# One decoder trunk step on one core: last up products stored after one tile load, three word gathers per two row gathers, a fourth row buffer, the residual read back in four larger transfers

## The reference

```python
s1, i1 = lax.top_k(s[:, :, 0], 16); s2, i2 = lax.top_k(s[:, :, 1], 16)   # 8 heads, 128 keys a side
...                                                    # the best 16 of the 256 pairs of a head
act = jax.nn.gelu(jnp.einsum('cd,chkd->chk', hc, expert_u[idx]))
return jnp.einsum('chk,chkd->cd', gate * act, expert_v[idx])
```

## Time and profile before

| | us |
|---|---|
| median of 3 runs (lowest, highest) | 2215.64 (2212.16, 2217.15) |
| the profiled execution's own time | 2217.63 |
| its span, first to last instruction | 2215.9 |
| TensorE busy | 2166.3 (98%), x16578 |
| VectorE busy | 1620.5 (73%) |
| ScalarE busy | 1120.8 (51%) |
| GpSimd busy | 785.4 (35%) |
| mean granted TensorE clock | 0.988 of full speed |

### The profile page before, as it was taken

How to read it: one execution, slowest core, us unless ns; L and a number is a source line. 1 busy time by engine, 2 the same in 40 slices (tenths; PEclk the granted TensorE clock), 3 DMA queues, 4 the chain that set the end, 5 groups by cost and what they waited for, 6 DMA issues and landing times.

```text
span 2215.9 us, 53111 instructions
## 1 busy us (share of the span) xinstructions
PE 2166.3 (98%) x16578; PEld 2128.9 (96%) x16578; DVE 1620.5 (73%) x2983; ACT 1120.8 (51%) x2094; POOL 785.4 (35%) x612
## 2 busy tenths in 40 slices
PE   9999999999999999999999999999889999999997
PEld 8999899999999999999999999999789999999997
DVE  8778688886766767888885444466567787788886
ACT  6445366667455445555555444455333444444453
POOL 0321100002011000888888888200577433222231
PEclk9999999999999999999999999999999999999998
DMA  7887656666556556877776878698899999899995
GB/s 245 292 292 248 224 185 199 207 210 209 182 187 204 176 173 182 192 179 190 189 185 179 204 185 188 179 314 260 273 320 307 350 390 379 313 369 371 369 365 191
DMA packets 303834, 546.01 MB, mean 246 GB/s; under 512 B 77072, under 2 KB 116456, under 8 KB 303600
## 3 DMA queue, kind: packets, MB, share of 16 engines
q1 hardware_dynamic: 227024, 427.68, 59.6%
q0 software_dynamic: 60064, 105.07, 16.0%
q10 hardware_dynamic: 16640, 12.06, 1.8%
HBM read 519.39 MB, written 25.28 MB: 246 GB/s over the span
## 4 chain that ended last, share of the span: by engine, by line
PE 65%; POOL 5%; issue 3%; DMA 2%; DVE 2%; ACT 0%; DVEq 0%; SPq 0%; ACTq 0%
PE ps L317 15%; PE ps L320 15%; PE ps L316 15%; PE ps L2207 8%; PE ps L2220 5%; PE ps L2211 5%; POOL gu L1790 3%; DMA gat<-expert_v,gidx 2%; POOL gat L1639 1%; DVE lo L1623 0%; PE ps L2251 0%; DMA raw<-weights 0%; PE ps L1403 0%; DMA gu<-u_spill,gidx 0%; DVE gacc L2085 0%
## 5 line engine op out<-in xcount | busy, mean ns | idle before, releaser
L304 DVE TENSOR_TENSOR lo<-raw,hi 128x512 fp32r<-128x512 f32 x995 | 685.8, 697 | 365.6 <-ACT hi L299 345.0
L299 ACT CAST hi<-raw 128x512 fp32r<-128x512 f32 x995 | 608.1, 620 | 471.9 <-PE ps L320 447.2
L316 PE MATMUL ps<-h_hi,hi 128*128 128x264 f32 (+1 forms) x3200 | 821.8, 286 | 1.0 <-DVE h_lo L957 1.0
L317 PE MATMUL ps<-h_lo,hi 128*128 128x264 f32 (+1 forms) x3200 | 820.1, 286 | 0.0
L316 PEld LDWEIGHTS ps<-h_hi,hi 128*128 128x128 f32 x3200 | 601.8, 188 | 7.9 <-issue 6.3
L317 PEld LDWEIGHTS ps<-h_lo,hi 128*128 128x128 f32 x3200 | 602.0, 188 | 0.3 <-issue 0.2
L1773 POOL DMA_INDIRECT w_spill<-chosen,widx x256 | 432.4, 1689 | 264.5 <-DVE widx L1998 186.8
L320 PE MATMUL ps<-h_hi,lo 128*128 128x264 f32 (+1 forms) x3200 | 523.3, 285 | 2.1 <-DVE lo L304 1.9
L320 PEld LDWEIGHTS ps<-h_hi,lo 128*128 128x128 f32 x3200 | 444.3, 188 | 3.8 <-DVE lo L304 3.6
L2207 PE MATMUL ps<-whl,hi 128*128 128x368 f32 x1544 | 348.7, 348 | 6.4 <-DVE whl L2077 5.2
L1639 POOL DMA_INDIRECT gat<-expert_v,gidx x160 | 178.0, 1112 | 315.4 <-DVE gacc L2085 297.4
(11 more groups left out here) (308 smaller groups left out, 2294.4 us busy)
## 6 DMA issues: line engine op xcount, KB each, us to landing
raw<-u_tiles SPq DMA_DIRECT2D x512, 256.0 KB
raw<-weights SPq DMA_DIRECT2D x480, 256.0 KB
raw_v<-expert_v SPq DMA_DIRECT2D x128, 512.0 KB
raw<-expert_v SPq DMA_DIRECT2D x124, 512.0 KB
w_spill<-zeros ACTq DMA_DIRECT2D x16, 736.0 KB, 5.6
wld<-w_spill SPq DMA_DIRECT2D x32, 368.0 KB, 4.1
u_spill<-ust SPq DMA_DIRECT2D x128, 40.0 KB
qb<-q_spill POOLq DMA_DIRECT2D x8, 512.0 KB, 5.9
```

Source lines behind the costliest of these rows:

```text
L299: nc.scalar.copy(hi[k % SPLIT][:], raw_quarter(k)).then_inc(hi_done, 1)
L304: nc.vector.tensor_tensor(lo[k % SPLIT][:], raw_quarter(k), hi[k % SPLIT][:].bitcast(F32), ALU.subtract).then_inc(lo_done, 1)
L316: pe.matmul(out, a, rhs[0][:, first + j, 0:n], start=start and j == 0, stop=False)
L317: pe.matmul(out, a, rhs[1][:, first + j, 0:n], start=False, stop=False)
```

## The change

- SyncE stores the last up products behind the load of tile 4 of round 0, ahead of those of tiles 5 to 7.
- A fourth row buffer `gat3`, over the third cell buffer of `wld`; row n goes out when add n-4 is done. Before row 3, the first into that buffer, GpSimd waits until VectorE's multiplications of the up pass are done.
- GpSimd's list: five words; then two words behind each of rows 0 to 4; from row 5 one behind an odd row and two behind an even one.
- Five batches of words: up to word 5, 15, 30, 50, 80, weighed ahead of rounds 1, 2, 4, 7, 10.
- Adds of the first pass: round 1 has four (behind k=3, 5, 6, 7), rounds 2 to 7 five, rounds 8 to 13 six, 14 and 15 five.
- The residual comes back in four transfers of 528 KB: one behind the loads of round 1's tiles, one behind round 2's, two behind round 3's.
- Five semaphores that are only counted up become one, `go`.

```diff
+    gat3 = place("gat3", at["raw_v"] + 2 * 4 * 4 * TD, [P, HALF * P])
+    gacc = place("gacc", at["gat3"], [P, len(GROUPS), HALF * P])
...
-    gat.append(gat2)
+    gat += [gat2, gat3]
+    ROWS = len(gat)
...
-    BOUNDS = (1, 3, 6, 9)
+    BOUNDS = (1, 2, 4, 7, 10)
     FIVE, SIX = (1, 2, 3, 5, 6), (1, 2, 3, 5, 6, 7)
-    ADDS = [[()] + 7 * [FIVE] + 4 * [SIX] + [SIX, FIVE, FIVE, (0, 1, 2, 3, 4)], 15 * [FIVE] + [(0, 1, 2, 3, 4)]]
+    ADDS = [[(), (3, 5, 6, 7)] + 6 * [FIVE] + 6 * [SIX] + [FIVE, (0, 1, 2, 3, 4)], 15 * [FIVE] + [(0, 1, 2, 3, 4)]]
+    WORDS_AT = (0, 5, 15, 30, 50, TG)
...
-        for s in range(RAW, SLOTS):
+        def x2_back(q):
+            at_q = slice(4 * q, 4 * q + 4) if isinstance(q, int) else bass.ds(4 * q, 4)
+            sp.dma_start(x2[:, at_q], x2_dram[:, at_q]).then_inc(x2_in, 16)
+        load_expert(0, 0, RAW)
+        spill(PAIR_U - 1, 1)
+        for s in range(RAW + 1, SLOTS):
             load_expert(0, 0, s)
-        spill(PAIR_U - 1, 1)
...
-        sp.dma_start(x2[:, 0], x2_dram[:, 0]).then_inc(x2_in, 16)
-        sp.dma_start(x2[:, KD - 1], x2_dram[:, KD - 1]).then_inc(x2_in, 16)
-        for first, last in ((1, CHUNKS - UP_CHUNKS - 1), (CHUNKS - UP_CHUNKS - 1, NK // 8 - 1)):
...
+        x2_back(0)
+        with sp.Fori(1, CHUNKS - UP_CHUNKS - 1) as i:
+            for s in range(SLOTS):
+                load_expert(0, i + 1, s)
+                if s == 2:
+                    sp.wait_ge(w_mul, UP_CHUNKS + i + 4)
+                    cells_in(UP_CHUNKS + i + 1, 1)
+            x2_back(i)
+        x2_back(3)
+        with sp.Fori(CHUNKS - UP_CHUNKS - 1, NK // 8 - 1) as i:
+            for s in range(SLOTS):
+                load_expert(0, i + 1, s)
...
-        for n in range(TG):
-            if n >= 3:
-                pool.wait_ge(gat_used, n - 1)
-            gather_rows(n)
-            if n >= 2:
-                for _ in range(min(2, TG - words)):
-                    gather_u(words)
-                    words += 1
-        for n in range(TG, 2 * TG):
-            pool.wait_ge(gat_used, n - 1)
-            gather_rows(n)
-            if n == TG + 2:
+        for n in range(2 * TG):
+            if n == ROWS - 1:
+                pool.wait_ge(w_mul, UP_CHUNKS + 3)
+            if n >= ROWS:
+                pool.wait_ge(gat_used, n - ROWS + 2)
+            gather_rows(n)
+            for _ in range(min(1 if n > ROWS and n % 2 else 2, TG - words)):
+                gather_u(words)
+                words += 1
+            if n == TG + ROWS - 1:
                 pool.wait_ge(mm_done, 2 * C0 + 2 * NK + SPLIT)
                 nc.gpsimd.memset(gacc[:], 0.0).then_inc(gacc_zero, 1)
...
-            dve.wait_ge(gu_in[b], 16 * (WORD_TURNS[b + 1] - WORD_TURNS[b]))
+            dve.wait_ge(gu_in[b], 16 * (WORDS_AT[b + 1] - WORDS_AT[b]))
...
-                dve.wait_ge(x2_in, 16 * KD)
+                dve.wait_ge(x2_in, 16 * KD // 4)
```

More of the change, by code:

```diff
@@ L430, in program @@
     t_added, a_ready, o_ready, o_done = sem("t_added"), sem("a_ready"), sem("o_ready"), sem("o_done")
[L431 removed]
+    go = sem("go")
     NG = HEADS // GH
@@ L1304, in mid_gpsimd @@
                 pool.wait_ge(sq_used, CALL[2] + 2 * i + b)
-                pool.sem_inc(pool_go, 1)
+                pool.sem_inc(go, 1)
                 nc.gpsimd.tensor_tensor(acc2[:], acc2[:], work2[:, b, :], ALU.add).then_inc(sq_used, 1)
@@ L1529, in mid_vector @@
                 dve.wait_ge(norm_lo, CALL_N + j - 1)
-                dve.sem_inc(dve_go, 1)
+                dve.sem_inc(go, 1)
                 norm_scaled(x, work2, b, j, 1, rstd2, LIVE)
@@ L1548, in program @@
     sel_seen = sem("sel_seen")
-    gat_in, gat_used = [sem(f"gat_in{b}") for b in range(3)], sem("gat_used")
-    gu_in = [sem(f"gu_in{b}") for b in range(4)]
+    gat_in, gat_used = [sem(f"gat_in{b}") for b in range(4)], sem("gat_used")
+    gu_in = [sem(f"gu_in{b}") for b in range(5)]
     gw_made, gacc_zero = sem("gw_made"), sem("gacc_zero")
@@ L1578, in program @@
     G_FIRST = [sum(GROUPS[:g]) for g in range(len(GROUPS))]
-    WORD_TURNS = [-(-sum(len(a) for a in ADDS[0][:i]) // TURN) * TURN for i in BOUNDS] + [TG]
-    FIRST_WORDS = WORD_TURNS[1]
+    assert all(sum(len(a) for a in ADDS[0][:i]) <= n for i, n in zip(BOUNDS[1:], WORDS_AT[1:]))
     def column(n):
@@ L1788, in gather_u @@
         def gather_u(n):
-            j, batch = column(n), max(b for b in range(4) if n >= WORD_TURNS[b])
+            j, batch = column(n), max(b for b in range(len(BOUNDS)) if n >= WORDS_AT[b])
             nc.gpsimd.indirect_dma_start(gu[:, j:j + 1], None, u_rows,
@@ L1792, in gather_u @@
                 .then_inc(gu_in[batch], 16)
-        for n in range(FIRST_WORDS):
+        words = WORDS_AT[1]
+        for n in range(words):
             gather_u(n)
-        words = FIRST_WORDS
-        for n in range(TG):
-            if n >= 3:
-                pool.wait_ge(gat_used, n - 1)
-            gather_rows(n)
-            if n >= 2:
-                for _ in range(min(2, TG - words)):
-                    gather_u(words)
-                    words += 1
-        for n in range(TG, 2 * TG):
-            pool.wait_ge(gat_used, n - 1)
-            gather_rows(n)
-            if n == TG + 2:
+        for n in range(2 * TG):
[3 more added lines that the diff above has]
+                pool.wait_ge(gat_used, n - ROWS + 2)
+            gather_rows(n)
+            for _ in range(min(1 if n > ROWS and n % 2 else 2, TG - words)):
+                gather_u(words)
+                words += 1
+            if n == TG + ROWS - 1:
                 pool.wait_ge(mm_done, 2 * C0 + 2 * NK + SPLIT)
@@ L2080, in add_rows @@
         def add_rows(n):
-            j, b = column(n), n % 3
+            j, b = column(n), n % ROWS
             g = 0 if j < GROUPS[0] else 1
-            dve.wait_ge(gat_in[b], 16 * (n // 3) + 16)
+            dve.wait_ge(gat_in[b], 16 * (n // ROWS) + 16)
             dve.wait_ge(gat_used, n + 1)
@@ L2088, in weigh_rows @@
         def weigh_rows(b):
-            first, last = WORD_TURNS[b] // TURN, WORD_TURNS[b + 1] // TURN
-            dve.wait_ge(gu_in[b], 16 * (WORD_TURNS[b + 1] - WORD_TURNS[b]))
+            first, last = WORDS_AT[b] // TURN, WORDS_AT[b + 1] // TURN
+            dve.wait_ge(gu_in[b], 16 * (WORDS_AT[b + 1] - WORDS_AT[b]))
             for rows_of in (slice(first, last), slice(GROUPS[0] + (TURN - 1) * first, GROUPS[0] + (TURN - 1) * last)):
```

15 lines of the change are left out of this document (7 added, 8 removed).

## The result

| | before | after |
|---|---|---|
| median of the runs, us | 2214.0 (4 runs, 2212.16 to 2217.15) | 2189.63 (4 runs, 2188.6 to 2189.87) |
| span of the profiled execution | 2215.9 | 2186.9 |
| mean granted clock | 0.988 | 0.993 |

The ratio is 0.9888, with a 95% interval from 0.987 to 0.9905: 24.4 us less, where 18.0 were forecast and 2197.6 for the time. The sign and the place were right; the forecast gain was a quarter too small, and the time lies 3.4 us under the forecast's own range of 2193 to 2202.

The account below looks back on a forecast made before the run. The gathers one GpSimd queue can issue bound the first down pass's first half. 20.0 us gained by round 10's k=3, 12.9 of it by round 1's, less 2 for crowding: 18.0 off 2215.64 gives 2197.6; range 2188 to 2209.

Parts of the forecast that it names:

- The first hole: Ahead of round 1: earlier store starts GpSimd 9.8 us earlier, first weighing's wait goes, round 1's k=3 12.9 us sooner.
- rival 1: First down pass: the transfers bind; at 330 GB/s gain 12.1 us, time 2203.5, at 313 no change; chance 0.22.
- signs of being wrong: Late rows with GpSimd waiting for adds, gathers of 1.6 us or more, TensorE waiting for tiles, second pass moving.
- Row 4: In GpSimd's list, row 4 waits for add 0 at k=3 of round 1, which ends at 1579.1.
- A gather's price: GpSimd's list up to word 79: 1.25 us a gather plus 0.70 an add, 169.6 us for 111 gathers and 44 adds.
- The last wait: Ahead of round 10: VectorE waits for the last word, landed at 1756.3; k=3 at 1761.2 against 1781.17, 20.0 us gained.
- the 2 us for crowding: Round 1's to round 10's k=3: tiles or rows late in rounds with residual parts; 2 us lost, between 0 and 18.5.
- behind round 10: Four rounds of six adds against three cost 1.0 us more, fewer residual bytes give 1.4; taken at 0, -2 to +2.
- The fourth buffer at 0.8 us up to there: First half of the first down pass: the fourth buffer alone is worth at most the 0.8 us of waiting.
- The slower one: GpSimd's gathers held up by a fuller VectorE, 1.80 us each, time 2227.8; decides from 1.69 us a gather; chance 0.05.
- Rival 3: Ahead of round 1: early store lands late among tile loads, GpSimd starts at 1563.0 as before; 2202.7; chance 0.06.
- Rival 4: More gain: 1.483 us a gather, 3.4 us behind the last wait, nothing crowded; 26.2 us, time 2189.4; chance 0.12.

Follow-up runs that it names:

- short adds: The changed kernel with each add on 16 of its 1024 columns, the others left out; executed once, 2185.94 us.
- Six batches: The changed kernel with a sixth batch of words ending at word 65 and fewer words behind a row from row 15 on; 2177.15 us, ratio 0.9832.

## Why the prediction was right, and where it was short

- **The first hole.** Store at 1548.7 (1547.93), GpSimd from 1553.2 (1551.94), no wait at the first weighing: right. Round 1's k=3 at 1574.6 was 3.9 us too early (1578.49), and the slow clock did not go whole: it was 0.60 from 1574.8 to 1578.5. I took TensorE's 1.25 us at 1568.56 as all that would stay. With the hole gone, the round's tiles became the next thing late: ScalarE waited for tiles (3.57, 2.39, 4.08 and 2.93 us) and TensorE 3.73, with four rows gathered in the same stretch. From 1568 to 1574 us the transfers moved 396 GB/s. This is rival 1, at this one place, and TensorE waiting for tiles was one of the signs of being wrong. The rows have a part in it: sent later they bring that k=3 to 1574.90. No order that was tried makes the whole faster.
- **Row 4.** I had it at 1579.2 behind a wait of 4.7 us; it was 1583.89 behind 8.65, since add 0 hangs on that late round.
- **A gather's price.** 111 gathers and 44 adds were to take 169.6 us; from 1583.89 to 1750.56 they took 166.7, 1.50 each. The price of 0.70 an add came out at 0.63 by the same sum ((166.7 - 0.3 - 138.8) / 44). That all of it belongs to the adds was wrong: some 60% does, and the rest to VectorE's other instructions. The Trainium skill (SBUF — State Buffer, "SBUF: two separate sides") describes a gather's descriptors held up by VectorE's instructions in a 2-port mode; one with two inputs in SBUF contends, as it says, only with a GpSimd instruction that reads SBUF, and a `tensor_tensor` was not seen there to stall a DMA. The adds and the subtractions have two such inputs, the subtractions are of that kind, and gathers beside them lasted up to 1.99 us in the changed kernel and 1.91 with short adds, against 0.95 beside a still VectorE. That fits a lock, and for the subtractions the measurement decides against the page; which access of a gather meets the lock no run here shows.
- **The last wait.** The last word was to land at 1756.3 and VectorE to stand before it: it stood 7.61 us, until 1754.55, and round 10's k=3 came at 1760.35 (1761.2 forecast, 1763.2 with the 2 us for crowding). That this is so near is in part luck: the terms were off by +4.7 us (row 4), -3.5 (170.2 us with the wait for add 1, 166.7 measured), -2.9 (the last word landed 4.0 us after its issue, not 6.9) and +0.9 (5.8 us behind the wait, not 4.9). The crowding cost nothing by that point, because what it cost was hidden in that wait. Six batches show it: with the wait gone, 2.9 us over TensorE's own pace are left between the two marks.
- **The term that was mis-sized: behind round 10.** I set it to 0 between -2 and +2, and it was 5.0. I had read the 1.0 us a round of six adds as the work's own and asked only how many such rounds there are, and gave the residual's bytes 1.4 us. It was VectorE waiting for rows at 3.07 us a row with three buffers, and the fourth takes it away: 113.9 us with three in the changed kernel, 105.0 with four, and 105.0 with four in the kernel before. The residual has no part: with it back in 16 parts the stretch still takes 105.0.
- **The fourth buffer at 0.8 us up to there** was drawn from waits of the list of before, which was too long to be held by buffers. Alone it gave 3.6; in the new, shorter list its absence costs (11.93 + 193.89) - (14.55 + 181.86) = 9.4 us by round 10's k=3.
- **Rivals.** The slower one (1.69 us a gather) was far off at 1.50. Rival 3, no use for the early store, was wrong for the kernel before (9.9 us); in the changed one the store gives 1.6, within the noise, for a reason that it did not name. Rival 4 gave 2189.4, almost the 2189.63 that was measured, and that is luck: its 2 us for a pass without crowding came back by round 10 and its gather of 1.483 us nearly held (1.50), but behind the last weighing it had 3.4 us where 5.5 were measured, and it had nothing for the 5.0 behind round 10.
- **The sum.** Between the profiled executions 29.0 us were gained, not 18.0: 2.8 more by round 10's k=3, 5.0 behind it, 3.2 in the last stretch. The last is hardly the change's: the execution of before was 3.6 us over its median (I had allowed 2.0) and the one of after 1.0 under, which brings 29.0 to 24.4.

## What to carry to other kernels

When two kinds of work share one in-order list, ask for each batch boundary which item of the list it waits for and what stands ahead of that item: the 12.5 us that the change left lay in the reach of one batch, not in any engine's pace. A buffer's worth is read from the list that will run: it was 9 us in the old list, 15.6 in the new. And the parts of a change don't add up: the store and the buffer alone give 9.9 and 9.1 us, taken out of the whole they cost 1.6 and 15.6. The new list without the fourth buffer gives nothing beyond the early store (2205.19 with both, 2204.96 with the store alone). The new list alone, and the store and the buffer together with the old list, were not run, so what the list adds to these two stays open. A cost per round that TensorE's marks show is not the work's own until the waits within the round are read.

## What was not expected of the hardware

- From 1587 to 1667 us the transfers of the changed kernel moved 386 to 396 GB/s while words were gathered; the 346 GB/s at which I drew the crowded case was no limit.
- Matmuls behind TensorE's long waits ran at the 1.2 GHz level. In the changed kernel the granted clock was 0.60 from 1574.8 to 1578.5 us, behind a wait of 3.73 us, and 0.55 from 1755.6 to 1760.3, behind one of 8.99; in the kernel before it stayed at 1.00 from 1568.6 to 1570.0, behind one of 1.25. Ahead of round 10 the 8.99 us wait cost 11.4 us in all (20.61 against 9.23).
- A gather took 0.95 us beside a still VectorE even with the transfers at 403 GB/s, and up to 1.91 us beside a working one, the adds being cut to 16 columns.
